# Moving weight and source splits, and two reciprocals, within the queues of a two-block transformer kernel

## The reference

```python
def conv_ffn(h, w_up, conv_w, conv_b, w_down):
    u = h @ w_up                                   # 1024 -> 2 x 2816
    up = jnp.pad(u, ((0, 0), (1, 1), (0, 0)))
    u = up[:, :-2] * conv_w[0] + up[:, 1:-1] * conv_w[1] + up[:, 2:] * conv_w[2] + conv_b
    a, b = jnp.split(u, 2, axis=-1)
    return (jax.nn.silu(a) * b) @ w_down           # 2816 -> 1024
...
for l in range(L_):                                # one layer
    h = _rms(x, mix_norm_g[l])
    p = h @ w_in[l]                                # latent attention and hyena inputs
...
    x = x + _mem_xattn(_rms(x, cross_norm_g[l]), _rms(mem, mem_norm_g[l]), w_mq[l], w_mkv[l], w_mo[l])
    x = x + _hier_moe(...)                         # 32 experts
```

## Time and profile before

| | us |
|---|---|
| runs | 2700.99, 2688.69, 2701.23 |
| median | 2700.99 |
| span of the profiled execution | 2686.4 |
| PE busy | 2508.4 (93%) |
| VectorE (DVE) busy | 1351.7 (50%) |
| ScalarE (ACT) busy | 868.8 (32%) |
| GpSimd (POOL) busy | 283.6 (11%) |

### The profile page before, as it was taken

How to read it: one execution, slowest core, us unless ns; L and a number is a source line. 1 busy time by engine, 2 the same in 40 slices (tenths; PEclk the granted TensorE clock), 3 DMA queues, 4 the chain that set the end, 5 groups by cost and what they waited for, 6 DMA issues and landing times. The chain is left out here.

```text
span 2686.4 us, 35719 instructions
## 1 busy us (share of the span) xinstructions
PE 2508.4 (93%) x15040; PEld 1940.8 (72%) x15040; DVE 1351.7 (50%) x2188; ACT 868.8 (32%) x1400; POOL 283.6 (11%) x230
## 2 busy tenths in 40 slices
PE   7999989999999899999899999998988999998976
PEld 5887558888887788897669999774744578763322
DVE  3323554666666313423647777337566755533213
ACT  3224443333334112324444333224331643320001
POOL 0501420000000000302500000000032120011112
PEclk9999999999999999999999999999999999999999
DMA  6113731111111112224512222420200114359997
GB/s 248 51 61 121 249 122 48 63 63 63 63 63 33 54 65 69 73 69 166 185 49 93 83 92 91 150 95 16 80 27 9 48 63 136 131 201 368 421 421 293
DMA packets 56672, 322.25 MB, mean 120 GB/s; under 512 B 8061, under 2 KB 14333, under 8 KB 24573
## 3 DMA queue, kind: packets, MB, share of 16 engines
q1 hardware_dynamic: 44510, 299.11, 30.2%
q0 software_dynamic: 5696, 12.59, 1.2%
q10 hardware_dynamic: 6304, 8.23, 0.9%
HBM read 315.71 MB, written 12.58 MB: 122 GB/s over the span
## 5 line engine op out<-in xcount | busy, mean ns | idle before, releaser
L978 PE MATMUL ps<-work_rounded,ring_rounded 128*128 128x512 f32 (+1 forms) x2016 | 535.0, 353 | 12.9 <-DVE ring_rounded L883 4.9
L978 PE MATMUL ps<-xn_rounded,ring_rounded 128*128 128x512 f32 (+2 forms) x2304 | 540.7, 347 | 0.0
L2090 PE MATMUL ps<-xn_rounded,ring_rounded 128*128 128x258 f32 (+2 forms) x2816 | 532.9, 311 | 0.0
L2090 PEld LDWEIGHTS ps<-xn_rounded,ring_rounded 128*128 128x128 f32 x2816 | 412.9, 190 | 30.9
L978 PEld LDWEIGHTS ps<-xn_rounded,ring_rounded 128*128 128x128 f32 x2304 | 371.8, 190 | 57.5 <-issue 0.2
L978 PEld LDWEIGHTS ps<-work_rounded,ring_rounded 128*128 128x128 f32 x2016 | 334.1, 191 | 72.1 <-DVE work_rounded L397 7.6
L978 PE MATMUL ps<-big_rounded,ring_rounded 128*128 128x512 f32 (+1 forms) x1200 | 319.8, 357 | 19.4 <-DVE ring_rounded L883 14.6
L883 DVE TENSOR_TENSOR ring_rounded<-ring,ring_rounded 128x2048 fp32r<-128x2048 f32 (+3 forms) x106 | 191.9, 1812 | 268.2 <-ACT ring_rounded L848 268.2
L2090 PE MATMUL ps<-work_rounded,ring_rounded 128*128 128x256 f32 (+1 forms) x1232 | 279.1, 308 | 5.7 <-DVE ring_rounded L2141 4.2
L848 ACT ACTIVATE ring_rounded<-ring 128x2048 fp32r<-128x2048 f32 (+3 forms) x106 | 160.5, 1517 | 315.2 <-PE ps L978 289.7
L978 PEld LDWEIGHTS ps<-big_rounded,ring_rounded 128*128 128x128 f32 x1200 | 198.3, 191 | 59.7 <-DVE ring_rounded L883 16.7
(11 more groups left out here) (426 smaller groups left out, 3126.4 us busy)
## 6 DMA issues: line engine op xcount, KB each, us to landing
ring<-in_stream SPq DMA_DIRECT2D x141, 1024.0 KB, 4.8
big<-in_experts SPq DMA_DIRECT2D x44, 1024.0 KB, 26.0
ring<-in_stream SPq DMA_DIRECT2D x32, 704.0 KB, 4.1
ring<-in_experts SPq DMA_DIRECT2D x22, 1024.0 KB, 26.7
xn<-in_experts SPq DMA_DIRECT2D x15, 1024.0 KB, 28.7
work<-in_experts SPq DMA_DIRECT2D x15, 1024.0 KB, 29.0
big<-in_first_modulation SPq DMA_DIRECT2D x8, 1024.0 KB, 14.2
work<-in_bias ACTq DMA_DIRECT2D x20, 256.0 KB, 4.3
```

The costliest lines, as they stand in the source:

```text
L978: mm = pe.matmul(out[:, a - u.first:b - u.first], lhs, rhs, start=j == 0 and n == 0 and not u.onto, stop=j == terms - 1 and n == len(passe ...
L2090: mm = pe.matmul(out[:, a:b], ws[:, k, :], x[k][:, a - base:b - base], start=k == 0 and n == 0, stop=k == KT - 1 and n == 2)
```

## The change

Five edits, all of order; no arithmetic is added or removed.

1. Down splits its second strip ahead of source 9 (`early=9`), not behind all sources.
2. The feed-forward splits both halves of strip 1 ahead of the root and the reciprocal, not the first alone.
3. In the second projection the reciprocal for the first norm goes behind unit 3's eviction, and ScalarE skips its waits for evictions in units 0 to 3 (`add_from=HY`).
4. In the memory projection the eight stream sources are split one by one behind units 2 to 9 (`late`), and `early` falls away.
5. There, too, the stream's reciprocal goes behind unit 11's eviction.

```diff
@@ PairNorm.on_vector
         settle(dve, dve.reciprocal(self.rstd, self.rstd), vstep)
-        dve.wait_ge(rooted.sem, rooted.at(2))
-        settle(dve, dve.reciprocal(self.first_rstd, self.first_rstd), vstep)
+
+    def invert_first(self, dve):
+        b = self.b
+        dve.wait_ge(b.sig("rooted").sem, b.sig("rooted").at(2))
+        settle(dve, dve.reciprocal(self.first_rstd, self.first_rstd), b.sig("vector_step"))
@@ MemoryNorm.on_vector
-        for n, root in enumerate((self.rstd[0], self.token_rstd, self.rstd[1])):
+        for n, root in enumerate((self.rstd[0], self.token_rstd)):
             dve.wait_ge(b.sig("rooted").sem, b.sig("rooted").at(n + 1))
             settle(dve, dve.reciprocal(root, root), b.sig("vector_step"))
+
+    def invert_stream(self, dve):
+        b = self.b
+        dve.wait_ge(b.sig("rooted").sem, b.sig("rooted").at(3))
+        settle(dve, dve.reciprocal(self.rstd[1], self.rstd[1]), b.sig("vector_step"))
@@ project (new arguments: add_from=0, late=range(0))
-            for k in range(tiles_ahead, len(sources)):
+            for k in range(tiles_ahead, len(sources) - len(late)):
                 if k == early and following < 2:
                     split_strip(following)
                     following += 1
...
                 take(i)
+                if i in late:
+                    split_tile(len(sources) - len(late) + i - late[0])
...
                 def take(i):
-                    if add:
+                    if add and i >= add_from:
                         if not units[i].carry:
                             act.wait_ge(taken.sem, taken.at(evicted[i]))
                         add(act, i)
@@ ffn_up, ScalarE
-                high(1, 0)
+                for c in range(2):
+                    high(1, c)
                 deferred.root(act, products[1][1])
                 for i, c in halves_of:
-                    if i + 1 < FT and (i, c) != (0, 0):
+                    if 1 <= i < FT - 1:
                         high(i + 1, c)
@@ ffn_up, VectorE
-                low(1, 0)
+                for c in range(2):
+                    low(1, c)
                 deferred.invert(dve)
                 dve.wait_ge(zeroed.sem, zeroed.at(1))
                 for j, (i, c) in enumerate(halves_of):
-                    if i + 1 < FT and j >= 1:
+                    if 1 <= i < FT - 1:
                         low(i + 1, c)
@@ ffn_down
-        self.project(units, 2 * KT, finish, banks_each=2, sources=sources, tiles_ahead=tiles_ahead,
+        self.project(units, 2 * KT, finish, banks_each=2, sources=sources, tiles_ahead=tiles_ahead, early=9,
@@ second_projection
         def after(dve, i):
             t = i - HY - 1
+            if i == HY - 1:
+                norm.invert_first(dve)
...
-        self.project(units, 8, finish, sources=norm.rooms, deferred=norm, tiles_ahead=PAIRED_AHEAD, add=add, after=after, waiting=(0, 1))
+        self.project(units, 8, finish, sources=norm.rooms, deferred=norm, tiles_ahead=PAIRED_AHEAD, add=add, after=after, waiting=(0, 1),
+                     add_from=HY)
@@ memory_attention
-        self.project(units, 12, finish, sources=norm.rooms, deferred=norm, early=KT, tiles_ahead=KT)
+        def after(dve, i):
+            if i == 11:
+                norm.invert_stream(dve)
+
+        self.project(units, 12, finish, sources=norm.rooms, deferred=norm, tiles_ahead=KT, late=range(2, 2 + KT), after=after)
```

More of the change, by code:

```diff
@@ L902, in project @@
     def project(self, units, strips, finish, sources, banks_each=1, prefetch=None, deferred=None, add=None, gpsimd=None,
-                early=None, following_strip=False, loads=None, following_halves=False, after=None, beside=None, tiles_ahead=0, waiting=(0, 0)):
+                early=None, following_strip=False, loads=None, following_halves=False, after=None, beside=None, tiles_ahead=0, waiting=(0, 0),
+                add_from=0, late=range(0)):
         first = len(self.freed_at)
```

## The result

The changed kernel takes 2656.9 us, median of 6 runs (2653.93 to 2664.18), beside 2694.84 for 6 runs of the kernel before in the same comparison (2682.44 to 2704.5). The ratio is 0.9874, with an interval of 0.9847 to 0.9901: faster by 1.3%. The forecast was 2671, from 2657 to 2689. The profiled executions went from a span of 2686.4 us to 2652.8, so 33.6 less; the run profiled after took 2654.65, 1.85 above its span.

What follows compares the result with a forecast made beforehand. The prediction took TensorE, busy 2508.4 of 2686.4 us, as the bound, held up by late strips; 10.5 + 2.1 + 2.0 + 3.9 + 5.7 + 5.4 = 29.6 us off the median 2700.99 gave 2671, range 2657 to 2689.

Steps and rivals of the forecast that it cites:

- The places and the mechanism: Six PE stalls, together 22.8 us, each from one strip queued behind work needed later; low clock behind four adds 7.7.
- Down, layer 0: Down's first unit: stall of 7.90 us and clock loss of 2.6 go, a gain of 10.5 us.
- The margin of 0.35 us: Layer 0's down: source 9's low part, split behind the moved strip, is ready 0.35 us before PE needs it.
- Down, layer 1: Wait of 2.40 us goes with no clock term, less 0.3 for a new wait: gain 2.1 us.
- The new wait for the filters' loads: Down, layer 1: PE, arriving earlier, waits for filter loads, dft last; between 0 and 2.4 us, taken as 0.3.
- Feed-forward: Both layers' half-strip stalls go: gain 2.0 us in layer 0, 3.9 in layer 1 including 1.7 of clock.
- The drain: Feed-forward: the Trainium skill's 1.38 us behind a table load would cost 0.5 us in layer 1; not counted.
- Second projection: Second block's projection, fifth unit: stall of 4.03 us and clock loss of 1.7 go, a gain of 5.7 us.
- Memory projection: Fifth unit: stall of 4.34 us and clock loss of 1.7 go, less a new 0.6 at strip 7: gain 5.4.
- (A): Rival: only idleness goes, other places lose the clock, thin margins fail; gain 19 us, 2682; chance 0.18.
- (B): Rival: gain absorbed later because the experts' weights pace the last part; 2701, within 0.5%; chance 0.11.
- (C): Rival: feed-forward VectorE starts its round 1.5 us late and never catches up; slower, 2723; chance 0.04.

Runs made afterwards that it cites:

- the last kernel: The changed kernel with the stream's reciprocal behind unit 12 instead of 11 and a semaphore of its own for the dft load: 2655.74 us, ratio 0.9882.
- position 18: The changed kernel with down's second strip in layer 0 ahead of source 18 instead of 9: 2658.39 us.
- the sources alone: The kernel before with the memory projection's eight stream sources split behind units 2 to 9, its reciprocal left in the old place: 2674.47 us.
- the half strips alone: The kernel before with only both half strips split ahead of the feed-forward's root: 2678.97 us.
- the one with two fillers: The kernel before with dummy matmuls at two PE waits, 8 in layer 0's down, 5 half-width in layer 0's context attention: 2683.16 us, ratio 0.9988.
- down alone: The kernel before with only down's second strip split ahead of source 9, in both layers: 2686.17 us, ratio 0.9961.
- ScalarE's waits alone: The kernel before with only ScalarE's waits for evictions in units 0 to 3 of the second projection left out: 2700.33 us.
- the memory projection's both edits: The kernel before with only the memory projection's sources split late and the stream's reciprocal behind unit 11: 2698.92 us.
- position 2: The changed kernel with down's second strip in layer 0 ahead of source 2 instead of 9: 2673.43 us.

## Why the prediction was right, point by point

- **The places and the mechanism.** Right in all six: each stall was one strip behind work that is needed later, and went when its edit was made alone (in the second projection when both were).
- **Down, layer 0.** 10.5 predicted, 10.6 in the comparison and 10.6 again with the edit alone. The margin of 0.35 us held. Nine is a good position, though not a knife's edge: two makes the unit 1.1 us longer, and eighteen 6.4.
- **Down, layer 1.** The mis-sized term: 2.1 predicted, 1.3 measured. The new wait for the filters' loads was set at 0.3 within 0 to 2.4. It was 1.19 here, and 1.0 to 1.5 in the kernels that keep it:

```profile
1669.72 1.07 PE L466 MATMUL ps<-work,vec 33*64 33x512 f32 x2 [1.19 <-DMA work<-in_dft]
```

  Why it was too low: I reasoned that strip 3 and nothing else lay behind dft in the queue, and took the landing for nearly done. It ends by its own time, though, and of 2.4 us by which PE came earlier half was spent waiting for it. When PE no longer asks for dft there, the wait is gone and 1.3 us come back, which shows this to be the cause.
- **Feed-forward.** 2.0 and 3.9 predicted, 2.2 and 3.9 measured, with no later half strip late. The drain that would have cost 0.5 us in layer 1 was not there. That the clock's 1.7 us fell in layer 1 and not in layer 0 is luck of the profile of before: the same two stalls stand in other profiles with the loss in both layers, and in one with none in either (last section).
- **Second projection.** 5.7 predicted, 4.4 measured over the stretch. The stall of 4.03 and the low clock behind it went, and with both edits alone strip 2 was ready 1.4 us ahead of PE, as worked out. From the start of the stretch to PE's wait for `xn` it was 104.4 us and is 98.6 with both edits alone, at both other positions and in the last kernel: 5.8 less, the term as predicted. In the changed kernel it is 100.2, because PE lost the clock at another place, ahead of the fifth unit and right behind the wait at line 533. First before, then after:

```profile
1870.79 1.98 PE L533 MATMUL ps<-xn,base 128*128 128x512 f32 x4 [0.97 <-DVE xn L547]
```

```profile
1847.22 3.61 PE L533 MATMUL ps<-xn,base 128*128 128x512 f32 x4 [2.12 <-DVE xn L547]
```

  The same matmuls take 1.6 us longer; the granted clock is 0.68 in the 5 us from 1847.30 on, where before it is 1.00. At position 18 that wait is 2.12 us too, and the clock held. Over the whole stretch the changed kernel and the three built on it, all with the same code there, took 354.8, 354.2, 350.9 and 355.9 us, so that a single profile of the whole doesn't tell 4.4 from 5.7.
- **Memory projection.** 5.4 predicted, 5.4 measured, with 0.5 for the stall set at 0.6. The step that credited the moved reciprocal was wrong in its sense, though not in the sum: the sources alone give 5.7.
- **Rivals.** (A) would have given 19 us; the edited stretches gave 27.9, and the low clock behind their stalls went with them. Once, at line 533, another place did lose the clock instead, for 1.6 us. Its thin margins didn't fail either, except the filters' loads by half. (B) is refuted by the table's last row: the tail takes 371.6 us instead of 371.8, so it starts earlier by all that was gained. (C) is refuted by the half strips alone.
- **The size of the total.** 2656.9 lies 0.1 us below the lower bound of the range as written (2657), and 14 us under the forecast. The gain was sized well: 29.6 predicted, 27.9 in the edited stretches, and 34 by the ratio, within 27 to 41. What was off is the time that it was taken from. The median of three runs, 2700.99, was high; over all 48 runs of before made in this study it is 2686.2, and 2686.2 - 29.6 = 2656.6. The gain under the shortest run, which the prediction worked out as 2659, was the nearer one. The bound is mis-summed too: the gain with another 1 us under the shortest run is 2688.69 - 30.6 = 2658.1, and the measured time lies 1.2 us below that. That the time still comes out at the edge of the range is owed to this slip and not to the working. Chance had its part on both sides: two of the three runs were among the 15 of 48 over 2699, and none of the six of the changed kernel took over 2665, where two of six of the last kernel took over 2671.

## What to carry to other kernels

Price a late buffer at its stall and at the low clock behind it: here the strip stalls of 4 us and more cost 1.6 to 3.0 us on top in every profile, those of some 2 us either 1.7 or nothing, from run to run. Then ask of every instruction ahead of the late one when its own reader wants it, and move only what is needed later. Where PE comes earlier, look at the first thing it asks of a DMA that was loaded with no spare time: the gain stops there. Judge a change of 1% by stretches cut at the same instructions, because the total carries the whole kernel's variation.

## What the runs showed of the hardware that I had not expected

**A long stretch at the low clock while PE is busy.** The first stretch, edited in no kernel but the one with two fillers, took 467 to 471 us in nine of the 14 profiled runs, 475.6 in that of before, and 490 in four (down alone, ScalarE's waits alone, the memory projection's both edits, position 2). The same window in down alone and in the changed kernel:

```profile
330.00:367.50 37.50, 37.50 (x210) 19.52 (x206) 9.36 (x37) 10.55 (x35) 0.00 (x0) 0.50 0.52 173
```

```profile
330.00:367.50 37.50, 32.81 (x376) 22.02 (x370) 18.29 (x63) 17.18 (x54) 10.72 (x6) 0.91 0.58 219
```

The first shows PE at 1.2 GHz for all 37.5 us though it is never idle; 18.75 us of it are lost, and 3.4 in the second. That makes most of the difference between 471 and 490: from the wait below to PE's next wait for line 1931 (1942 in the changed kernel) it is 57.5 us and 41.6, and the other 3.2 us lie ahead. PE had stood still just ahead of the stretch:

```profile
PE ps L1126 <- DVE work L1187: 2.4, 1, 2.4
```

The same wait stands also in runs in which the clock held. The Trainium skill ("TensorE: Matmul & The Clock Gate", What's actually happening) has activity release the throttle; behind down's stalls the traces agree, here a busy PE stayed throttled. It matches the 20 us between single runs: of the 48 runs of before 32 lie under 2691, 15 over 2699 and one between, and the last kernel has two of 6 over 2671 where the others are under 2660. That these are the runs with the long stretch is argued from the profiled ones, not shown for each.

The start of the kernel goes with it. The same matmuls, before and after:

```profile
18.32 1.93 PE L684 MATMUL ps<-big,work 128*32 128x256 f32 x16
```

```profile
18.01 1.07 PE L692 MATMUL ps<-big,work 128*32 128x256 f32 x16
```

Sixteen of this size take 1.93 us in the long stretch as well, where the granted clock is 0.50, so by their durations PE ran at 1.2 GHz here too in the profile of before. (Its clock column reads 1.00 at this place, but the first record of the clock is of 39.0 us there, and of 17.6 in the changed kernel.) From 18 to 38 us PE is busy for all 20.00 us in the profile of before and in the four, and for 12.4 to 15.5 in the nine others. Part of this is covered by the wait for line 397: it is 7.9 us in the changed kernel and 2.9 in before, where it ends 3.7 us later. That is most of the 4.2 us by which the first stretch differs in the table. And these five profiles are the only ones with a low stretch that begins at 329 to 330 us, of 10.2 us in that of before and 37.5 in the four. Whether the one brings about the other, or both have one cause, was not tried.

With dummy products ahead of the wait at line 1126, the profiled run has no such stretch, and none of the 12 runs took over 2688.54. But this profile is one of the nine with a quick start, and the eight others have no such stretch without any filler, so that it says nothing about them:

```profile
330.00:340.00 10.00, 10.00 (x96) 5.61 (x85) 4.32 (x18) 5.22 (x18) 0.00 (x0) 1.00 0.89 325
```

In that comparison, moreover, only 2 of 17 runs of before went over 2700, so that 12 without one would come by chance in about one case of five ((15/17) to the 12th is 0.22). Whether the fillers prevent the stretch stays open, and so does what decides, from run to run, if it comes.

**A stall need not cost the clock.** Of three stalls of 2.0 to 2.4 us, those in layer 0's feed-forward and in layer 1's down left the clock at 1.00 and the one in layer 1's feed-forward did not the earlier trace rows. That is no property of the places. Each stall stands untouched in nine profiles. In layer 0's feed-forward (2.01 us) the clock held in four, all with the slow start told above, and in five 1.7 us were lost (the stretch took 385.9 us instead of 384.4); in layer 1's (2.17) it was lost in eight and held in that of down alone (263.0 instead of 264.5); in layer 1's down (2.4) it held in eight and was lost in that of the half strips alone. The strip stalls of 4.0 to 7.9 us, the three found and the one of 4.43 that was made, cost it in every profile that has them. What decides between the short ones was not tried.
